# Attention values as the stationary operand, probabilities divided before they are turned, and a new spacing of the memory attention's steps

## What is computed

```
# branch c: 4 heads of 128, 256 memory rows, no mask
s = einsum('bshd,bmhd->bhsm', q, k) * 128**-0.5
p = softmax(s);   y_c = einsum('bhsm,bmhd->bshd', p, v)
# branch b: 8 heads, q and k of 96, v of 64, causal, 256 rows in two blocks of 128
s = einsum('bqhd,bkhd->bhqk', q, k) * 96**-0.5, masked
p = softmax(s);   y_b = einsum('bhqk,bkhd->bqhd', p, v)
merged = gate_a * (y_a @ w_a) + gate_b * (y_b @ w_b) + gate_c * (y_c @ w_c)
```

## Time and profile before

| | |
|---|---|
| median of 3 runs | 906.39 us (906.1 to 906.51) |
| the profiled execution, own time | 906.13 us |
| its span, first to last instruction | 904.4 us |
| PE busy | 892.2 us, 99% |
| DVE busy | 616.1 us, 68% |
| ACT busy | 463.6 us, 51% |
| POOL busy | 44.2 us, 5% |
| mean granted clock of TensorE | 0.997 |
| idle time of PE in 230:400 us put down to a wait | none |

### The profile page before, as it was taken

How to read it: one execution, slowest core, us unless ns; L and a number is a source line. 1 busy time by engine, 2 the same in 40 slices (tenths; PEclk the granted TensorE clock), 3 DMA queues, 4 the chain that set the end, 5 groups by cost and what they waited for, 6 DMA issues and landing times.

```text
span 904.4 us, 11264 instructions
## 1 busy us (share of the span) xinstructions
PE 892.2 (99%) x4208; PEld 745.1 (82%) x4208; DVE 616.1 (68%) x862; ACT 463.6 (51%) x695; POOL 44.2 (5%) x66
## 2 busy tenths in 40 slices
PE   8999999999999999999999999999999999999996
PEld 7788888888998888888888888887888788888885
DVE  6788876747558877597667777766768755555653
ACT  6665544536688466447545545345445444444440
POOL 0010000022103000000000000001000100000000
PEclk9999999999999999999999999999999999999998
DMA  9897778764554544444687877865655565555541
GB/s 360 317 335 279 278 276 288 268 229 153 175 180 165 184 165 163 165 172 157 226 287 280 278 276 278 286 226 176 244 186 177 182 222 187 186 187 186 183 143 47
DMA packets 56575, 197.83 MB, mean 219 GB/s; under 512 B 6936, under 2 KB 7880, under 8 KB 56392
## 3 DMA queue, kind: packets, MB, share of 16 engines
q1 hardware_dynamic: 55944, 196.19, 62.9%
q10 hardware_dynamic: 576, 0.92, 0.3%
HBM read 196.01 MB, written 1.07 MB: 218 GB/s over the span
## 4 chain that ended last, share of the span: by engine, by line
PE 94%; DMA 1%; issue 1%; SPq 1%; DVE 1%; POOL 1%; ACT 1%; POOLq 0%; ACTq 0%
PE ps L721 29%; PE ps L723 29%; PE ps L722 29%; PE ps L748 2%; DMA t_raw<-in_f_up 1%; PE ps L636 1%; PE ps L629 1%; PE ps L847 1%; PE ps L863 1%; SPq L1747 0%; PE ps L805 0%; PE ps L839 0%; POOL t_sc L1676 0%; PE ps L787 0%; POOL t_sc L1647 0%
## 5 line engine op out<-in xcount | busy, mean ns | idle before, releaser
L1196 DVE TENSOR_TENSOR t_wl<-t_raw,t_wh 128x1024 fp32r<-128x1024 f32 (+3 forms) x308 | 363.6, 1205 | 147.8 <-ACT t_wh L905 145.9
L905 ACT ACTIVATE t_wh<-t_raw 128x1024 fp32r<-128x1024 f32 (+3 forms) x308 | 310.6, 1041 | 144.0 <-DMA t_raw<-in_f_up 68.4
L721 PE MATMUL ps<-t_wh,t_XH 128*128 128x512 f32 (+2 forms) x640 | 250.8, 392 | 0.5 <-DVE t_hp L1317 0.5
L723 PE MATMUL ps<-t_wh,t_XL 128*128 128x512 f32 (+2 forms) x640 | 247.2, 386 | 0.0
L722 PE MATMUL ps<-t_wl,t_XH 128*128 128x512 f32 (+2 forms) x640 | 246.8, 386 | 0.0
L723 PEld LDWEIGHTS ps<-t_wh,t_XL 128*128 128x128 f32 x640 | 120.1, 188 | 24.2
L721 PEld LDWEIGHTS ps<-t_wh,t_XH 128*128 128x128 f32 x640 | 120.2, 188 | 23.3 <-issue 0.9
L722 PEld LDWEIGHTS ps<-t_wl,t_XH 128*128 128x128 f32 x640 | 120.3, 188 | 22.5
L721 PE MATMUL ps<-t_wh,t_YH 128*128 128x512 f32 x288 | 113.4, 394 | 0.0
L723 PE MATMUL ps<-t_wh,t_YL 128*128 128x512 f32 x288 | 112.2, 390 | 0.0
L722 PE MATMUL ps<-t_wl,t_YH 128*128 128x512 f32 x288 | 112.1, 389 | 0.0
(11 more groups left out here) (227 smaller groups left out, 625.9 us busy)
## 6 DMA issues: line engine op xcount, KB each, us to landing
t_raw<-in_f_up SPq DMA_DIRECT2D x131, 512.0 KB, 4.1
t_raw<-in_f_dn SPq DMA_DIRECT2D x66, 512.0 KB, 3.5
t_raw<-in_ada SPq DMA_DIRECT2D x48, 512.0 KB, 4.6
t_raw<-in_mkv SPq DMA_DIRECT2D x8, 512.0 KB, 3.7
t_raw<-in_ga SPq DMA_DIRECT2D x8, 512.0 KB, 3.2
t_raw<-in_gc SPq DMA_DIRECT2D x8, 512.0 KB, 3.2
t_raw<-in_gb SPq DMA_DIRECT2D x8, 512.0 KB, 3.3
t_raw<-in_wo SPq DMA_DIRECT2D x8, 512.0 KB, 3.2
```

Source lines behind the costliest of these rows:

```text
L721: pe.matmul(o, xh, h, start=k == 0, stop=False)
L723: x = pe.matmul(o, xl, h, start=False, stop=k == n - 1)
L905: act.activation(wh[:, m % SPL, lo:w], raw[:, n % RAW, lo:w], ACT.Copy).then_inc(hi_made, 1)
L1196: dve.tensor_tensor(wl[:, n % RAW, lo:w], raw[:, n % RAW, lo:w], wh[:, m % SPL, lo:w].bitcast(F32), ALU.subtract).then_inc(drained, 1)
```

## The change

The values become the stationary operand (`MV`, `VT`) and the turned probabilities move, so the result of `val` already lies turned. For the memory that is two matmuls with 256 moving columns in place of four with 128. For branch b it is three matmuls with 128 columns in place of 64: two heads' values (128 columns) are loaded, and the half of the result that belongs to the head is used. The division by the sums moves ahead of the turn: a new step `norm` at n-2, on DVE alone, takes the reciprocal and scales the probabilities in place (two instructions). After `val`, ACT copies the high part (one instruction for each head) and DVE subtracts for the low part; branch b has new tiles `YBH` and `YBL` in the space of `V` and `QM`. `y_turn` of `c` and `b` is gone. The memory's steps now hang on units 15, 17, 19, 22, 25, 28, 31, 33.

```diff
-        parts = (("mem_val", k - 4), ("mem_pt", k - 3), ("mem_sc", k - 1), ("mem_in", k), ("mem_exp", k - 1))
+        parts = (("mem_norm", k - 2), ("mem_val", k - 4), ("mem_pt", k - 3), ("mem_sc", k - 1), ("mem_in", k), ("mem_exp", k - 1))
...
-        parts = (("att_val", k - 4), ("att_pt", k - 3), ("att_sc", k - 1), ("att_in", k), ("att_exp", k - 1))
+        parts = (("att_norm", k - 2), ("att_val", k - 4), ("att_pt", k - 3), ("att_sc", k - 1), ("att_in", k), ("att_exp", k - 1))
...
-            30: [("row1", "k", 0), ("row3", "q", 0)], 31: [("row1", "k", 1), ("y_turn", "c", 0), ("y_turn", "c", 1)],
+            30: [("row1", "k", 0), ("row3", "q", 0)], 31: [("row1", "k", 1)],
...
-            61: [("y_turn", "b", 0), ("y_turn", "b", 1)]}
     for n in range(8):
-        side[15 + 2 * n] = side.get(15 + 2 * n, []) + mem(n)
+        k = (15, 17, 19, 22, 25, 28, 31, 33)[n]
+        side[k] = side.get(k, []) + mem(n)
...
             def mem_pt(h):
                 b = bank(("mem_pt", h), mpt_made, h + 1)
-                pe.wait_ge(mexp, 2 * h + 2)
+                pe.wait_ge(mnorm, h + 1)
...
             def mem_val(h):
-                b = bank(("mem_val", h), mval, 2 * h + 2)
+                b = bank(("mem_val", h), yc_lo, h + 1)
...
-                for t in (0, 1):
-                    for kt in (0, 1):
-                        m = pe.matmul(ps[:, b, t * P:t * P + P], mpT[:, (2 * t + kt) * P:(2 * t + kt) * P + P],
-                                      MV[:, kt, h * P:h * P + P], start=kt == 0, stop=kt == 1)
+                for kt in (0, 1):
+                    m = pe.matmul(ps[:, b, 0:256], MV[:, kt, h * P:h * P + P], mpT[:, kt * 256:kt * 256 + 256],
+                                  start=kt == 0, stop=kt == 1)
...
+                two = slice(h // 2 * P, h // 2 * P + P)
                 for t, kt, j in ((0, 0, 0), (1, 0, 1), (1, 1, 2)):
-                    m = pe.matmul(ps[:, b, t * 64:t * 64 + 64], pT[:, j * P:j * P + P], VT[:, kt, h * 64:h * 64 + 64],
+                    m = pe.matmul(ps[:, b, t * P:t * P + P], VT[:, kt, two], pT[:, j * P:j * P + P],
...
+            def mem_val(h):
+                b, full = place["mem_val", h]
+                act.wait_ge(turned, full)
+                act.activation(YH[:, 4 + h, :], ps[:, b, 0:256], ACT.Copy).then_inc(yc_hi, 1)
+
...
-            def mem_pt(h):
+            def mem_norm(h):
                 dve.wait_ge(mexp, 2 * h + 2)
                 dve.reciprocal(col("mrec", h, n=2), col("msum", h, n=2)).then_inc(*dve_chain.by())
+                dve.wait_ge(*dve_chain.now())
+                for t in (0, 1):
+                    p = mp[h % 2][:, t * 256:t * 256 + 256]
+                    m = dve.tensor_scalar(p, p, col("mrec", h, n=2)[:, t:t + 1], None, ALU.mult)
+                m.then_inc(mnorm, 1)
 
             def mem_val(h):
-                b, full = place["mem_val", h]
-                dve.wait_ge(turned, full)
-                dve.wait_ge(*dve_chain.now())
-                for t in (0, 1):
-                    dve.tensor_scalar(QM[:, t, h * P:h * P + P], ps[:, b, t * P:t * P + P],
-                                      col("mrec", h, n=2)[:, t:t + 1], None, ALU.mult).then_inc(mval, 1)
+                b = place["mem_val", h][0]
+                dve.wait_ge(yc_hi, h + 1)
+                dve.tensor_tensor(YL[:, 4 + h, :], ps[:, b, 0:256], YH[:, 4 + h, :].bitcast(F32), ALU.subtract).then_inc(yc_lo, 1)
```

More of the change, by code:

```diff
@@ L417, in build @@
             U = sb("U", [P, 2, 512], F32, c)
-            V = sb("V", [P, 2, 512], F32, c)
+            with ExitStack() as c2:
+                V = sb("V", [P, 2, 512], F32, c2)
+            YBH = sb("YBH", [P, 4, 256], F32R, c)
             ZQ = sb("ZQ", [P, 2, 384], F32, c)
             ZK = sb("ZK", [P, 2, 288], F32, c)
-            QM = sb("QM", [P, 2, 512], F32, c)
+            with ExitStack() as c2:
+                QM = sb("QM", [P, 2, 512], F32, c2)
+            YBL = sb("YBL", [P, 4, 256], F32R, c)
             MK = sb("MK", [P, 2, 512], F32, c)
@@ L541, in build @@
         qm_mean, qm_rstd = sem("qm_mean"), sem("qm_rstd")
-        mqk_made, mtop, mexp, mpt_made, mval = sem("mqk"), sem("mtop"), sem("mexp"), sem("mpt"), sem("mval")
+        mqk_made, mtop, mexp, mpt_made = sem("mqk"), sem("mtop"), sem("mexp"), sem("mpt")
+        mnorm, norm, yc_hi, yc_lo, yb_hi, yb_lo = (sem(n) for n in ("mnorm", "norm", "yc_hi", "yc_lo", "yb_hi", "yb_lo"))
         made_keys = steps("row1")
@@ L549, in build @@
         mixed, ya_made = sem("mixed"), sem("ya")
-        qkt_made, masked, top, expd, pt_made, val = sem("qkt"), sem("masked"), sem("top"), sem("exp"), sem("pt"), sem("val")
+        qkt_made, masked, top, expd, pt_made = sem("qkt"), sem("masked"), sem("top"), sem("exp"), sem("pt")
         y_keys = steps("y_turn")
@@ L646, in operands @@
                 if name[:2] == "br":
-                    return YH, YL, 4 if name[2] == "c" else 0
+                    return (YBH, YBL, 0) if name[2] == "b" else (YH, YL, 4 if name[2] == "c" else 0)
                 if name[:3] in ("mkv", "f2_") or name[:-1] == "co":
@@ L706, in mm @@
                     pe.wait_ge(parted, ring[{"uq0": "cq", "ukv0": "ckv"}[name], 2 * i] + 1)
-                if name in ("bra0", "brc0", "brb0") and t == 0:
-                    pe.wait_ge(*y_lo.at(name[2], i))
+                if name == "bra0" and t == 0:
+                    pe.wait_ge(*y_lo.at("a", i))
+                if name == "brc0" and t == 0:
+                    pe.wait_ge(yc_lo, 2 * i + 2)
+                if name == "brb0" and t == 0:
+                    pe.wait_ge(yb_lo, 4 * i + 4)
                 if name == "wo0" and i in (0, 2):
@@ L792, in mem_pt @@
                 b = bank(("mem_pt", h), mpt_made, h + 1)
-                pe.wait_ge(mexp, 2 * h + 2)
+                pe.wait_ge(mnorm, h + 1)
                 for j in range(4):
-                    m = pe.transpose(ps[:, b, j * P:j * P + P], mp[h % 2][:, j * P:j * P + P], ident[:, :])
+                    at = (j % 2 * 2 + j // 2) * P
+                    m = pe.transpose(ps[:, b, at:at + P], mp[h % 2][:, j * P:j * P + P], ident[:, :])
                 m.then_inc(turned, 1)
             def mem_val(h):
-                b = bank(("mem_val", h), mval, 2 * h + 2)
+                b = bank(("mem_val", h), yc_lo, h + 1)
                 pe.wait_ge(mpt_made, h + 1)
@@ L810, in y_turn @@
                 b = bank(("y", br, j), *y_lo.at(br, j))
-                src = QM if br == "c" else U
                 for t in (0, 1):
-                    if j == 0 and br == "c":
-                        pe.wait_ge(mval, 7 + t)
-                    if t == 0 and br == "a":
+                    if t == 0:
                         pe.wait_ge(ya_made, j + 1)
-                    if j == 0 and br == "b":
-                        pe.wait_ge(val, 15 + t)
-                    pair(b, src, t, 2 * j, t == 0)
+                    pair(b, U, t, 2 * j, t == 0)
             def su(s):
@@ L851, in att_pt @@
                 b = bank(("att_pt", h), pt_made, h + 1)
-                pe.wait_ge(expd, 2 * h + 2)
+                pe.wait_ge(norm, h + 1)
                 for j in range(3):
@@ L857, in att_val @@
             def att_val(h):
-                b = bank(("att_val", h), val, 2 * h + 2)
+                b = bank(("att_val", h), yb_lo, h + 1)
                 pe.wait_ge(pt_made, h + 1)
@@ L1082, in y_turn @@
                 act.wait_ge(turned, full)
-                k = (4 if br == "c" else 0) + 2 * j
+                k = 2 * j
                 act.activation(YH[:, k:k + 2, :], psum_2(b), ACT.Copy).then_inc(*y_hi.by(br, j))
@@ L1128, in att_pt, with att_val @@
                 act.activation(pT[:, :], ps[:, b, 0:384], ACT.Copy).then_inc(pt_made, 1)
+            def att_val(h):
+                b, full = place["att_val", h]
+                rows = slice(h % 2 * 64, h % 2 * 64 + 64)
+                if h == 0:
+                    act.wait_ge(ya_made, 2)
+                act.wait_ge(turned, full)
+                act.activation(YBH[rows, h // 2, :], ps[rows, b, 0:256], ACT.Copy).then_inc(yb_hi, 1)
             def gate(br, j):
@@ L1179, in _ @@
                     "nturn": nturn, "xturn2": xturn2, "evac": evac_, "lat_stat": lat_stat,
-                    "lat_turn": lat_turn, "mem_in": mem_in_, "mem_exp": mem_exp, "mem_pt": mem_pt, "y_turn": y_turn,
-                    "sv_sq": sv_sq, "row1": row1, "att_in": att_in, "att_exp": att_exp, "att_pt": att_pt, "gate": gate,
+                    "lat_turn": lat_turn, "mem_in": mem_in_, "mem_exp": mem_exp, "mem_pt": mem_pt, "mem_val": mem_val, "y_turn": y_turn,
+                    "sv_sq": sv_sq, "row1": row1, "att_in": att_in, "att_exp": att_exp, "att_pt": att_pt, "att_val": att_val, "gate": gate,
                     "mturn": mturn, "conv_gc": conv_gc, "conv_turn": conv_turn, "conv_gb": conv_gb,
@@ L1532, in att_sc, with att_norm, att_val @@
                                          op0=ALU.mult, op1=ALU.mult).then_inc(top, 1)
```

(19 more changed lines are left out.)

4 lines of the change are left out of this document (2 added, 2 removed), and 2 rows, old and new, of the table side.

## The result

| | before | after |
|---|---|---|
| median of 6 runs | 906.17 us (905.92 to 906.51) | 910.8 us (909.7 to 911.95) |
| the profiled execution, own time | 906.13 us | 910.87 us |
| its span | 904.4 us | 909.1 us |
| mean granted clock | 0.997 | 0.995 |

What follows compares the result with a forecast made beforehand. PE was taken as the bound, with ACT and DVE close behind where the change acts. PE's work -1.7, wait at `ukv0` +3.3 and at `u` +0.75 gave +2.4 us, a median of 908.8 us; range 905.3 to 910.4.

Steps and rivals of the forecast that it cites:

- steps 1 to 5: PE's own work: `y_turn` -1.7, memory's `val` -0.1, branch b's `val` +0.4, third head's `val` -0.1, `att_in` -0.17; sum -1.7 us.
- step 3: Branch b's `val` with 128 columns in place of 64: +0.05 us for each of eight heads, +0.4 us.
- X + 8.9: When exp of the memory's head 3 starts on ACT, in us counted from Gelu's table load.
- X + 10.5: When PE can start `ukv0`, counted from Gelu's table load; X + 6.1 before. Wait there 3.1 to 3.5, taken as 3.3 us.
- X: Start of Gelu's table load on ACT: forecast 259.1 us, spread 258.8 to 259.2; 261.92 before.
- The second wait: PE waits 0.75 us ahead of `u` for ACT's copies of `ukv0`, done at 277.1.
- B: Rival: both waits, and TensorE's clock falls: +0.5 to +1.0 us on A, twice that if longer; 909.3 to 911; chance 0.23.
- A: The forecast: waits at `ukv0` and `u`, clock unmoved: +1.9 to +2.9 us, 908.3 to 909.3; chance 0.36.
- C: Rival: DVE's backlog half as long, wait at `ukv0` 0.3 to 1.7 us, no second; 905.8 to 908.1; chance 0.17.
- D: Rival: no wait at `ukv0`, only DVE's chain to `att_in` binds: -0.9 us, 905.5; chance 0.15.
- E: Rival: PE's own sum alone: -1.7 us, 904.7; chance 0.04.
- My cover for branch b's `norm` at nothing: Branch b, units 37 to 61: `norm` priced at nothing; if cover failed, `att_pt` waits at most 0.6 us per head.

Runs made afterwards that it cites:

- e1: Changed kernel with exp of the memory's head 3 moved from unit 25 to 26, behind the copies of `uq0`: 907.46 us, ratio 1.0013.
- e9: Changed kernel with `norm` last, memory's steps at 15, 17, 19, 21, 25, 27, 29, 31, exp of head 3 at 26: 904.67 us, ratio 0.9981.
- e8: Changed kernel with `norm` at the end of each group of steps, behind the maxima, in both attentions: 907.02 us, ratio 1.0005.
- e2: Changed kernel with 28 unread transposes of the identity on PE between `uq1` and `ukv0`: 909.08 us, ratio 1.0032.
- e12: Changed kernel with 14 unread transposes of the identity on PE in the wait ahead of `ukv0`: 909.30 us, ratio 1.0034.
- e4: Kernel before with branch b's part of the change alone, the memory's attention as before: 906.46 us, ratio 1.0001.
- e5: Kernel before with the new spacing of the memory's steps alone, `y_turn` of c at unit 35: 909.05 us, ratio 1.0027.
- e13: The changed kernel once more, unchanged, against the kernel before on the same chip: 911.23 us, ratio 1.0054.

## Why the prediction was right or wrong

**The direction, the place and the mechanism were right.** PE stands ahead of `ukv0` and nowhere else in the mixer, for `uq0`'s copies behind exp(3); e1 and e9 take exp(3) away and the wait goes with it. Of eight table loads in the trace six were there before.

**PE's own work, steps 1 to 5: right.** `y_turn` is 0.87 shorter for c and 0.89 for b (0.86 each). The memory's four heads save 0.1, and the third `val`'s late copy and `att_in` give 0.16 and 0.18. For branch b the records of 128 columns stand (332.93 - 332.26)/6 = 0.11 apart, and the eight heads cost 0.38 (0.4). The estimate of 1.3 us from the Trainium skill's rule (TensorE: Matmul & The Clock Gate, Back-to-back issue gap), which I had set against step 3, is not what this trace shows; the row-based 0.4 is.

**X + 8.9 and X + 10.5: right; X: late by half a microsecond.** After the load (259.75), exp(3) begins 8.86 later and `ukv0` 10.54. X was to be 259.1; 0.19 of the difference is a slower start of the program in this execution, which moves PE too. The other 0.46 I had set at nothing: 0.33 lie ahead of exp(2), which began at 258.12, with a wait of DVE for POOL (0.18, between the two latent scalings) among them, and 0.13 between exp(2) and the load. So the wait was 3.8 and not 3.3, 0.3 over the end of my range of 3.1 to 3.5. The working did show that `norm` lies on that path, at 0.72 a head; e8 measures 2.15 for the three.

**The second wait: right where it could be seen.** Forecast 0.75 at `u`. In `after` it is missing, as B had it, because PE is late; in e2, where the clock stays up, it is 0.58, and in e8 0.59 (start to start).

**The step that failed is the choice between A and B, and B's size.** I gave "the clock unmoved" 0.36 and the fall 0.23, with the note that 3.3 us "may be enough". It was enough: two profiled executions out of two. And I priced the fall at "half of 2.4 to 3.5 us", +0.5 to +1.0 on A. Measured are 1.7 (against e2) and 1.8 to 1.9 (against e12). B's last words, "twice that if it lasts longer", do reach 911, but no row stood behind that length, and my range ended at 910.4. The halved length was the wrong one. I took the time that PE had worked at the program's start before the clock rose; here the clock was at 0.50 for 6.8 us. 5.2 us of that lay over work, which was twice as long as at 1.00 (the 12 passes: 5.24 for 2.8). The other 1.6 lay in the standstill and cost nothing. Half of 5.2 would be 2.6, nearly the 2.4 seen; less the second wait of 0.6 it is the net 1.8. The wait that was 0.5 too short doesn't take the forecast out of its range by itself: with the fall as I had priced it, it would be 909.8 to 910.3.

So the account of the profiled execution is: slower start +0.2, PE's own work -1.8, wait at `ukv0` +3.8, slower passes +2.4: +4.6, against 4.7 in the spans. The forecast's +2.4 lacks 2.2 of that: the clock makes up 1.8 (2.4 less the second wait), the longer wait 0.5, and the rest cancels to -0.1.

**C and D fell**: DVE's backlog was all there, and PE was at `ukv0` (266.5) as forecast (266.2). E fell with them, but e9 shows that it is what the change is worth once the order fits it. My cover for branch b's `norm` at nothing holds in `after` (no wait there); in e4 it failed in one head, by 0.61, the 0.6 that I had put beside it. The second added table load lies in the stretch where PE never waits; its price alone wasn't measured, but e9 has all eight loads and no new wait of PE.

## What to carry to other kernels

A step that is moved for the sake of its own distance crosses whatever stands between on every queue it uses: list those entries, and for each ask who waits for what was ahead. Here a result of one matmul row waited on ACT behind an exp that waited on DVE behind three scalings of another head. Put work that is due late (`norm`) behind work that is due now (the maximum): that one move was worth 3.8 us here (907.02 of e8 against 910.8), 2.15 of it in the wait and most of the rest in the clock that no longer fell. And a wait of PE has two prices; when it grew from 2 to 4 us here, the work behind it was done at half the clock. So a wait of such a length may be worth splitting even at the same total: e1 has 2.5 us of listed waits in two pieces and no fall, though no run here split one of 3.8 us at the same total.

## What the runs showed of the hardware that I had not expected

- One standstill of 3.8 us put the granted clock from 1.00 to 0.50 for 6.8 us, in both executions that were traced, of which 1.6 and 1.3 us still lay in the standstill: PE had stood for 2.2 and 2.5 us when it fell. Standstills of 1.65, 1.95, 1.96 and 2.3 us (e8, e5, e1, e12) didn't bring it down, each in one trace. None between 2.3 and 3.8 was tried.
- Transposes that compute nothing, put into the standstill, kept the clock up and gave back 1.7 us (e2), and half as many were as good (e12).
- fp32 matmul records of 64 and of 128 moving columns are almost the same distance apart, 0.11 us, in branch b; there a wider operand that saves transposes is nearly free.
- At the program's start PE works at half speed for a time that differs from one execution to the next, and the granted clock, which reads 1.00 there, doesn't show it; the distances do. In the traced execution of `before` pairs of 512-column passes are 0.46 us apart from the first weight product on (5.14 us); in that of `after` they are 0.86 apart until 8.81 and 0.46 only behind that. Between these two, waits for data take most of the difference up, and the mixers begin 0.2 us apart. But in e13, the same kernel as `after`, the pairs are 0.46 apart from 5.80 on, and its mixer begins 1.0 us sooner than in `after`: most of the spread between executions of one kernel may come from there, which wasn't tested by itself.
